# Queries, keys and values of tiles 4 to 7 made inside the loop's passes instead of in front, with other rings and buffers, in a one-core encoder block

## What is computed

```python
n1 = modulate(h, norm1_g, sh1, sc1)                  # 1024 tokens x 1024, RMSNorm and shift/scale from c
z, xbc, dtf, dtb, qkv, gate_ssd, gate_na = jnp.split(n1 @ w_in, IN_OFFSETS, axis=-1)
y_ssd = ssd_branch(z, xbc, dtf, dtb, ...) @ w_ssd_br # conv, chunked scan in both directions, gated RMSNorm
y_na = neighbourhood_attention(q, k, v, na_rpb) @ w_na_br   # 16 heads of 64, window 8 x 16 on a 16 x 64 grid
mixed = jax.nn.sigmoid(gate_ssd) * y_ssd + jax.nn.sigmoid(gate_na) * y_na
h = h + g1 * (mixed @ w_out)
n2 = modulate(h, norm2_g, sh2, sc2)
# PEER: 8 heads x 16 experts for each token, out of 16384 rows of 1024 floats in u and as many in v
h = h + g2 * einsum(gate * gelu(u[eidx] . n2), v[eidx])
```

## Time and profile before

| | before |
|---|---|
| median of 3 runs | 4299.2 us (4278.68 to 4303.11) |
| the profiled execution, its own time | 4317.7 us |
| its span | 4316.0 us |
| TensorE busy, mean granted clock | 2867.7 us, 0.811 |
| VectorE busy | 2480.9 us |
| GpSimd busy | 2102.6 us |
| ScalarE busy | 807.9 us |
| moved by DMA | 1389.46 MB |

### The profile page before, as it was taken

How to read it: one execution, slowest core, us unless ns; L and a number is a source line. 1 busy time by engine, 2 the same in 40 slices (tenths; PEclk the granted TensorE clock), 3 DMA queues, 4 the chain that set the end, 5 groups by cost and what they waited for, 6 DMA issues and landing times.

```text
span 4316.0 us, 41932 instructions
## 1 busy us (share of the span) xinstructions
PE 2867.7 (66%) x14107; PEld 1470.9 (34%) x14107; DVE 2480.9 (57%) x5249; ACT 807.9 (19%) x1840; POOL 2102.6 (49%) x2147
## 2 busy tenths in 40 slices
PE   5999998997766677795565767365568752333334
PEld 4887775543333333332232223132223320000000
DVE  4543447338575556547755565677556666666651
ACT  3323123211123211212232001121320110000000
POOL 1000313014564455656654556666555566666665
PEclk8999999999877888997687988677879876665556
DMA  8425754549998899999987999999899999999998
GB/s 212 66 65 172 227 169 153 196 177 378 393 322 323 294 403 406 405 407 377 371 332 286 403 405 405 406 355 366 308 347 404 402 392 364 372 369 368 377 367 333
DMA packets 503878, 1389.46 MB, mean 322 GB/s; under 512 B 65865, under 2 KB 136497, under 8 KB 502641
## 3 DMA queue, kind: packets, MB, share of 16 engines
q0 software_dynamic: 298768, 1086.75, 67.0%
q1 hardware_dynamic: 204896, 300.02, 20.2%
HBM read 1330.10 MB, written 56.51 MB: 321 GB/s over the span
## 4 chain that ended last, share of the span: by engine, by line
PE 21%; DMA 17%; POOL 13%; issue 12%; another core or an unknown queue 8%; DVE 7%; ACT 1%; SPq 0%; DVEq 0%; ACTq 0%; POOLq 0%
DMA ring<-in_peer_u,idx 13%; PE ps_l L1659 9%; POOL ring L2297 6%; POOL ring L2290 6%; PE acc L2519 4%; DVE junkF L2473 3%; DMA ring<-in_peer_v,idxT 2%; PE ps_l L1841 2%; PE ps_l L1887 1%; PE ps_l L1865 1%; DMA lane<-n_scr 1%; DMA gin<-zg_scr 1%; PE ps_l L1874 1%; PE ps_l L1734 1%
## 5 line engine op out<-in xcount | busy, mean ns | idle before, releaser
L2473 DVE CUSTOM_DVE_ANT_0 junkF<-ring,ps_n2F 128x1024 bf16<-128x1024 f32 x1024 | 1248.5, 1219 | 833.0 <-DMA ring<-in_peer_u,idx 585.1
L2297 POOL DMA_INDIRECT ring<-in_peer_u,idx x1024 | 1001.0, 978 | 877.3 <-DVE dots L2473 410.5
L2519 PE MATMUL acc<-ring,spread 128*32 128x512 f32 x4096 | 743.8, 850 | 911.7 <-DMA ring<-in_peer_v,idxT 772.1
L2290 POOL DMA_INDIRECT ring<-in_peer_v,idxT x1024 | 990.5, 967 | 705.3 <-PE acc L2519 286.8
L1659 PE MATMUL ps_l<-lane 128*128 128x512 f32 x1856 | 834.9, 604 | 41.7 <-DMA lane<-n_scr 18.8
L2519 PEld LDWEIGHTS acc<-ring,spread 128*32 128x32 f32 x4096 | 147.6, 138 | 1395.8 <-issue 1392.3
L1659 PEld LDWEIGHTS ps_l<-lane 128*128 128x128 f32 x1856 | 350.4, 193 | 499.4 <-issue 495.4
L1887 PE MATMUL ps_l<-ident,st 128*128 128x128 f32 x448 | 87.0, 327 | 181.5 <-ACT lane L1918 141.7
L2019 DVE CUSTOM_DVE_ANT_0 st<-ps_l,lane 128x512 f32<-128x512 f32 x96 | 66.3, 690 | 230.6 <-PE ps_l L1841 180.0
L515 POOL DMA_DIRECT2D bias<-rpb_scr x16 | 13.2, 829 | 325.5 <-PE ps_dt L801 279.8
L1841 PE MATMUL ps_l<-lane 128*128 128x512 f32 x192 | 134.6, 791 | 26.4 <-DVE nmax L2019 26.4
(11 more groups left out here) (354 smaller groups left out, 3980.9 us busy)
## 6 DMA issues: line engine op xcount, KB each, us to landing
lane<-in_peer_wq SPq DMA_DIRECT2D x16, 2048.0 KB
lane<-in_w_in SPq DMA_DIRECT2D x14, 2048.0 KB
w_z<-in_w_in SPq DMA_DIRECT2D x16, 1024.0 KB, 6.1
adaB<-in_w_ada SPq DMA_DIRECT2D x16, 1024.0 KB
lane<-in_w_na_br SPq DMA_DIRECT2D x8, 2048.0 KB
lane<-in_w_ssd_br SPq DMA_DIRECT2D x8, 2048.0 KB
lane<-in_w_out SPq DMA_DIRECT2D x8, 2048.0 KB
ring<-in_peer_u,idx POOLq DMA_INDIRECT x1024
```

Of the source, the lines that this page charges most:

```text
L2290: pool.indirect_dma_start(v_rows[:, nv % RV, :], None, a["peer_v"][0], bass.IndirectOffsetOnAxis(ap=idxT[:, m % 2, col:col + 1], axis=0)). ...
L2297: pool.indirect_dma_start(u_rows[:, n % RU, :], None, a["peer_u"][0], bass.IndirectOffsetOnAxis(ap=idx[:, i % RI, j:j + 1], axis=0)).then_ ...
L2473: nc.vector.tensor_tensor_reduce(out=junk[:, :], in0=u_rows[:, n % RU, :], in1=ps_n[:, :], scale=1.0, scalar=0.0, op0=ALU.mult, op1=ALU.ad ...
L2519: last = nc.tensor.matmul(acc[q * QUAD:(q + 1) * QUAD, cols], spread[:, m % 2, c0:c0 + QUAD], v_rows[:, nv % RV, cols], start=(g == 0 and ...
```

## The change

In front, the values are made for tiles 0 to 3 only (8 items instead of 16) and the queries and keys for the first 512 tokens only (one half of 24 matmuls for each of the 16 blocks, and a store of 512 columns instead of 1024). What is missing becomes "mul" jobs of the loop's gate stages: in pass 1 the keys and values of tiles 4 and 5 (8 jobs, 4 weight blocks, and one more load of a normed tile), in pass 2 the queries of tiles 4 and 5 and the keys and values of tiles 6 and 7 (12 jobs, 6 blocks), in pass 3 the queries of tiles 6 and 7 (4 jobs, 2 blocks). Each job ends with a ScalarE copy and a 256 KB store in rows of 128 floats. Queries and keys are computed transposed, as 32 matmuls of 128 columns.

Four other things change. The first block of the SSD's x moves into `stage_condition`, between the steps that make `n1`; that stage has six rooms for w_ada instead of eight and two PSUM buffers instead of three. In the recurrence, the scaling of `ps_off` (one VectorE instruction, L1800) and the addition to y (one, L1809) leave VectorE: ScalarE does the first in 8 instructions of 64 columns and the second as a copy, and TensorE adds y itself by one more matmul. `junk` is gone: a dot product writes its products over its own u row and no longer waits for the one before. `prod`, `off` and `qrow` share a room with `st`, and the freed memory makes `RV` 11. The last steps of a tile (`finish_sum`, `finish_norm`) are spread over more slots.

With the same rule the slots become: pass 1 gate 14 to 84, recurrence 84 to 123, attention 123 to 174; pass 2 gate 244 to 328, recurrence 328 to 369, attention 369 to 426; pass 3 recurrence 572 to 616, attention 616 to 677.

```diff
+                ps_x0 = banks(front, "ps_x0", 2)
+                split_room = ExitStack()
+                x_order = [[opener(split_room)(f"w_x_{part}{i}", [P, KD, P], f32r) for part in ("hi", "lo")] for i in range(2)]
...
-        ada = sb("ada", [P, KD, 2 * DM])
+        ada = sb("ada", [P, ADA_ROOMS, 2 * DM])
...
+                    if k >= ADA_ROOMS:
+                        sp.wait_ge(ada_sum, ada_room(k) + 1)
+                    sp.dma_start(ada[:, ada_room(k), :], w_ada[:, k, 0:2 * DM]).then_inc(s_ada[k], 16)
+                for b in range(2):
+                    sp.dma_start(w_first[b], w_in[:, :, COL_XBC + b * P:COL_XBC + (b + 1) * P]).then_inc(s_wx[b], 16)
...
+                for b in range(2):
+                    act.wait_ge(s_wx[b], 16)
+                    nc.scalar.activation(x_order[b][0][:, :, :], w_first[b], ACT.Copy).then_inc(x_hi, 1)
...
-                v.wait_ge(sq_done, TT)
-                nc.vector.tensor_scalar(rstd[:, :], sumsq[:, :], 1.0 / DM, EPS, ALU.mult, ALU.add).then_inc(mean_done, 1)
-                v.wait_ge(sqrt_done, 1)
-                nc.vector.reciprocal(rstd[:, :], rstd[:, :]).then_inc(rstd_done, 1)
                 v.wait_ge(cT_done, 2)
                 for k in range(KD):
+                    if k == 1:
+                        v.wait_ge(sq_done, TT)
+                        nc.vector.tensor_scalar(rstd[:, :], sumsq[:, :], 1.0 / DM, EPS, ALU.mult, ALU.add).then_inc(mean_done, 1)
...
+                for k in range(KD + 3):
+                    if k == 2:
...
+                    q = k - 3
+                    if q >= 0:
+                        if q == 0:
+                            pe.wait_ge(x_lo, 1)
+                        pe.wait_ge(hi_done, q + 1)
+                        pe.wait_ge(lo_done, q + 1)
+                        for h in range(2):
+                            last = exact_products(nc, ps_x0[:, h * HALF:(h + 1) * HALF], lambda part, i: x_order[0][part][:, i, :],
+                                                  lambda part, i: n1[part][:, i, h * HALF:(h + 1) * HALF], [q])
...
+                last.then_inc(x_mm, 1)
...
-    GATE_BLOCKS = [(3, i, COL_V + i * HALF, ACT.Copy, TT) for i in range(2)]
+    GATE_BLOCKS = [(3, i, COL_V + i * HALF, ACT.Copy, TT // 2) for i in range(2)]
...
-                    sp.dma_start(qk_scr[b * P:(b + 1) * P, :], row[:, b % 2, :]).then_inc(s_row[b % 2], 16)
+                    early = slice(0, HALF)
+                    sp.dma_start(qk_scr[b * P:(b + 1) * P, early], row[:, b % 2, early]).then_inc(s_row[b % 2], 16)
...
-                for b in range(XBC_BLOCKS):
+                for b in range(1, XBC_BLOCKS):
...
-                    for half in range(2):
+                    for half in range(1):
...
-    RU, RV, RI = 6, 10, 2
+    RU, RV, RI = 6, 11, 2
...
-        junk = sb("junkF", [P, DM], bf16)
...
-        st_room = sb("st", [P, RS * (GRID_W + HALF)])
+        st_room = sb("st", [P, (RS + RQ) * HALF])
         st = st_room[:, 0:RS * HALF].rearrange("p (r n) -> p r n", r=RS)
-        probs = st_room[:, :].rearrange("p (r n) -> p r n", r=RS)
-        prod = sb("prod", [P, HALF])
-        qrow = sb("qrow", [P, RQ, HALF])
+        probs = st_room[:, 0:RS * (GRID_W + HALF)].rearrange("p (r n) -> p r n", r=RS)
+        prod = st_room[:, (RS - 1) * HALF:RS * HALF]
+        qrow = st_room[:, RS * HALF:].rearrange("p (r n) -> p r n", r=RQ)
         qcol = sb("qcol", [P, RQ, 4, P])
         lstat = sb("lstat", [P, 4])
         nmax = sb("nmax", [P, 2])
...
+        KEYED = {(2, 3): (4, 5), (4, 5): (6, 7)}
...
-                    + [("load", t) for t in held[SETS:]] + [("mul", "gate", c, t) for c in range(4) for t in gated])
+                    + [("mul", "query", c, t) for c in range(2) for t in tiles if t >= TT // 2]
+                    + [("load", t) for t in held[SETS:]] + [("mul", "gate", c, t) for c in range(4) for t in gated]
+                    + [("load", t) for t in KEYED.get(tiles, ()) if t not in held]
+                    + [("mul", what, c, t) for what in ("key", "value") for c in range(2) for t in KEYED.get(tiles, ())])
...
+                for k in [k for k, m in enumerate(st_jobs) if m < OPEN_AT[a_pass]][-RS:]:
+                    stored_wait(sp, k)
...
-                c, t = JOBS[n][2:]
-                sp.dma_start(zg_scr[1 + c // 2, t * P:(t + 1) * P, c % 2 * HALF:(c % 2 + 1) * HALF], st[:, k % RS, :]).then_inc(s_gst[k % RS], 16)
+                what, c, t = JOBS[n][1:]
+                dst, src = zg_scr[1 + c // 2, t * P:(t + 1) * P, c % 2 * HALF:(c % 2 + 1) * HALF], st[:, k % RS, :]
+                if what == "value":
+                    dst = v_scr[c * PAIRS // 2:(c + 1) * PAIRS // 2, :, t, :].rearrange("r q n -> q r n")
+                elif what in ("query", "key"):
+                    d0 = (DM if what == "key" else 0) + c * HALF
+                    dst = qk_scr[d0:d0 + HALF, t * P:(t + 1) * P].rearrange("(r q) n -> q r n", q=P)
+                if what != "gate":
+                    src = src.rearrange("q (r n) -> q r n", n=P)
+                sp.dma_start(dst, src).then_inc(s_gst[k % RS], 16)
 
...
+                if what in ("query", "key"):
+                    cols = slice(part * P, (part + 1) * P)
+                    for k in range(KD):
+                        last = nc.tensor.matmul(bank[:, cols], w[:, blk % RW, k, cols], inT[:, f % SETS, k, :], start=(k == 0), stop=(k == KD - 1))
...
+                pe.wait_ge(d_scaled, 3 * (t - SOON + 1))
+                y = tok[:, tok_of[turn_at(t, "y", 0)] % RT, :]
+                nc.tensor.matmul(ps_y, ident[:, :], y[:, g * GP:(g + 1) * GP], start=True, stop=False)
                 pe.wait_ge(d_offr, u + 1)
                 for d in range(2):
-                    nc.tensor.matmul(ps_y, ident[:, :], off[:, d * GP:(d + 1) * GP], start=(d == 0), stop=False)
+                    nc.tensor.matmul(ps_y, ident[:, :], off[:, d * GP:(d + 1) * GP], start=False, stop=False)
...
+            elif kind == "soff":
+                if u % (2 * GROUPS) == 0:
+                    for m in [m for m, n in enumerate(st_jobs) if n < JOBS.index(("soff", t, g))][-RS:]:
+                        stored_wait(act, m)
+                act.wait_ge(d_off, u + 1)
+                if u:
+                    act.wait_ge(d_y, u)
+                for d in range(2):
+                    for h in range(HPG):
+                        cols, col = slice(d * GP + h * HEADDIM, d * GP + (h + 1) * HEADDIM), d * SH + g * HPG + h
+                        last = nc.scalar.activation(off[:, cols], ps_off[:, cols], ACT.Copy, scale=tabs[:, t % 2, col:col + 1])
+                last.then_inc(d_offr, 1)
+            elif kind == "sy":
+                act.wait_ge(d_y, u + 1)
+                y = tok[:, tok_of[turn_at(t, "y", 0)] % RT, :]
+                nc.scalar.activation(y[:, g * GP:(g + 1) * GP], ps_y, ACT.Copy).then_inc(d_yr, 1)
...
+                if u:
+                    v.wait_ge(d_y, u)
...
-            elif kind == "sy":
-                v.wait_ge(d_y, u + 1)
-                v.wait_ge(d_scaled, 3 * (k + 1))
-                nc.vector.tensor_tensor(y[:, cols], y[:, cols], ps_y, ALU.add).then_inc(d_yr, 1)
...
+                what = JOBS[n][1]
+                if what == "gate":
+                    nc.scalar.activation(st[:, k % RS, :], bank, ACT.Sigmoid).then_inc(p_act, 1)
+                else:
+                    nc.scalar.activation(st[:, k % RS, :], bank, ACT.Copy, scale=-(HEADDIM ** -0.5) if what == "query" else 1.0).then_inc(p_act, 1)
...
-                            if n:
-                                v.wait_ge(u_used, n)
-                            nc.vector.tensor_tensor_reduce(out=junk[:, :], in0=u_rows[:, n % RU, :], in1=ps_n[:, :], scale=1.0, scalar=0.0,
+                            nc.vector.tensor_tensor_reduce(out=u_rows[:, n % RU, :], in0=u_rows[:, n % RU, :], in1=ps_n[:, :], scale=1.0, scalar=0.0,
...
-                        if i >= 1 and j == FIN_SLOT + 5:
+                        if i >= 1 and j == SQUARE_SLOT:
+                            finish_square(i - 1)
+                        if i >= 1 and j == NORM_SLOT:
...
+        SQUARE_SLOT, ROOT_SLOT, NORM_SLOT = FIN_SLOT + 3, FIN_SLOT + 4, FIN_SLOT + 7
```

More of the change, by code:

```diff
@@ L173, in ev_count, with evicted, ada_room @@
         def ev_count(k, by_act):
-            return sum((i % 3 == 1) == by_act for i in range(k + 1))
+            return sum((i % 2 == 1) == by_act for i in range(k + 1))
+        def evicted(engine, k):
+            engine.wait_ge(ev_act if k % 2 else ev_dve, ev_count(k, k % 2 == 1))
+        def ada_room(k):
+            return k if k < ADA_ROOMS else k - ADA_ROOMS + 1
         with nc.Block() as block:
@@ L334, in stage_front @@
             xT = sb("xT", [P, 2, SEQ])
-            x_order = [[sb(f"w_x_{part}{i}", [P, KD, P], f32r) for part in ("hi", "lo")] for i in range(RS)]
             x_parts = [[x_order[i][part] for i in range(RS)] for part in range(2)]
@@ L362, in stage_front @@
```

(7 more changed lines are left out.)

104 lines of the change are left out of this document (52 added, 52 removed).

## The result

The changed kernel takes **4340.5 us** (median of 4 runs, 4314.0 to 4363.6) against 4291.1 for the kernel before (4 runs, 4278.7 to 4303.1): ratio 1.010, 95% interval 1.0057 to 1.0143. Measured a second time (experiment 6), with 6 runs against 11, the same pair gave 1.0086 (1.0064 to 1.0108). I had forecast 4260 and a range of 4190 to 4330. The change is slower, and the forecast and its sign were wrong.

The account below looks back on a forecast made before the run. The prediction took the front as bound by TensorE and the loop by DMA; front -121 and loop +82 gave -39 us on the profiled 4317.7, 4278.7, hence 4260 us against the runs' median, range 4190 to 4330.

Parts of the forecast that it names:

- Values: Front: 8 items of 24 matmuls go, 192 x 0.2346 us, taken in full since TensorE is the bound: -45 us.
- First block: Front: the SSD x's first 48 matmuls fill gaps between the steps that make n1: -12 us (0 to -14).
- Queries and keys: Front's query loop: 384 matmuls leave, stage falls from 196.5 to 132 us: -64; ends -95 (TensorE bound), -30 (loads in turn).
- Bytes: Loop: 32.0 MB more of weight blocks, stores and one load cost DMA time: +90 us (79 to 110).
- TensorE: Loop's gate stages: 24 jobs bring TensorE level with DMA, so waits for each other show: +30 us (0 to +70).
- slots: Loop: attention loses 16 slots to gate stages, where each costs 0.7 us more: +12 us.
- The wait between dot products: Recurrence and attention: idling up to 0.30 us before dot products goes; a third of at most 88 us taken: -30 us.
- the 11th place: Loop's last window: GpSimd runs one v row further ahead, winning idle DMA time: -12 us (0 to -42).
- the recurrence: Recurrence stages: VectorE loses L1800 and L1809, ScalarE gets nine instructions instead: -8 us.
- rival A: Loop: 110 us of idle DMA time come back instead of 50, so the front's gain stays whole: 4200 us; chance 0.24.
- Rival B: Gate stages: SyncE's queue, with new stores in 512-byte rows, delays weights TensorE needs: slower, 4335 us; chance 0.14.
- Rival C: Front: query loop stays at 165 us, held by the load behind 1 MB of w_ada: 4293 us; chance 0.15.

Follow-up runs that it names:

- experiment 6: On one chip against the kernel before: the change again 1.0086; with 10 v-row places instead of 11, 1.0069; with the recurrence's offset product back on VectorE, 1.0124.
- experiment 7: The change with an eighth of each moved weight block loaded, 0.9933 of the kernel before; with two of eight matmuls per moved job, 1.0027.
- experiment 3: The change with queries, keys and values all back in front, 0.9952 of the kernel before; the same with ScalarE's copy before the split, 0.9939.
- experiment 2: The change with only the first eighth of each w_ada block in the query loop loaded and summed; single run, that stage 143.9 us, 185.0 in the change.
- experiment 1: The change with ScalarE copying query block b out before splitting block b + 2; 0.9993 of the kernel before, 4311.2 against 4318.9 us.

## Why the prediction was wrong, step by step

- **Values, -45:** right, -42.3. **First block, -12 (0 to -14):** -15.6; the next stage starts earlier by that. Right in kind, a little more than its end.
- **Queries and keys, -64 (ends -95 and -30): this step failed.** It was -17.9. I wrote "124 us, more than TensorE's 101, and I take 132, since the loads wait for one another in SyncE's order", and took as the bad end that "each block waits for its 1.5 MB in turn", at -30. That end is what happens, and it costs more than I gave it: 9.3 to 14.6 us a block, from one load's issue to the next. What I did not follow is ScalarE's order, by which the store, and with it the next load, waits for a later block's load. In the kernel before it was covered by some 11 us of matmuls a block (48 of 831 in 190.23 us), with 7 us of waits for a late split in all; halving the matmuls took the cover off, and TensorE's pauses between blocks came to 65 us. With the two lines swapped the stage took 140.6 us, 62 below before's 202.9: that is the -64. Of the 58 us missed, 46 are here and 12 in the loop; the rest nearly cancels (values +3, first block -4, the stages behind the query loop -2, the end +3).
- The rule of the Trainium skill ("DMA: Bandwidth & Descriptors", Specifications) that I had set against this, line rate at 512 bytes and more, is not borne out by this case. In the change's trace a packet of 512 bytes takes 27 ns (median), one of 1024 46, one of 2048 84 and one of 4096 160, so the shortest rows move at three quarters of the rate of the longest. The mended stage is at a share of 0.90 with only 256 GB/s, against 405 in gate stages; part of that is GpSimd's bias traffic, whose 4096-byte packets take 247 ns on average there. The -95 was out of reach besides: TensorE alone is busy 109 us in the mended stage.
- **Bytes, +90:** +83 in packet time; right. **TensorE, +30 and slots, +12:** pass 1's gate stage came to 248.9 us, I had said 225; its idle DMA time, against a share of 1.03, went from 6 to 31 us, so a cost of that size is there. But three quarters of the products left out bring only 12 us of the loop (experiment 7); that the rest is late loads is shown at one place and not summed up.
- **The wait between dot products -30, the 11th place -12, the recurrence -8: the sum of 50 failed.** Recurrences and attentions took 1091.1 us over 319 slots before and 1032.2 over 293 after. The 26 slots fewer are worth 59 us at the prediction's own 2.0 and 2.7 us a slot, and 59 is the difference: nothing is left for the three terms. The place gives nothing; wait and offset are perhaps 15 each by the times, with intervals that reach nearly down to nothing, and with nothing moved all the other parts together leave some 7 us in the loop (experiment 3). All three rest on one sentence: that the 178 us below a share of 1.03 are lost to late engines. Most are not, and the DMA engines' idle time grew by 13 us where the prediction's terms had it shrink by 8 (30 + 12 - 50).

To see that, the throughput in 5 us slices from 3700 to 3900 us, of the change and of experiment 2, whose code is the same there:

```profile
DMA  8999997999999799999999789999989999997999
GB/s 328 358 392 419 408 410 251 305 379 415 404 407 411 255 336 382 345 409 380 410 412 408 257 274 381 415 408 410 412 308 295 419 409 407 412 387 245 317 411 411
```
```profile
DMA  9999999999999999999899999999999999999999
GB/s 407 410 413 406 407 410 401 403 410 409 406 410 414 407 408 410 410 388 356 309 337 417 413 411 407 410 410 410 408 410 410 407 408 409 409 408 412 409 410 407
```

Where the change was profiled the flow breaks down to some 250 GB/s about every 35 us; on the faster chip once in the 200. There the attention of pass 2 and the last window read:

```profile
2070.00:2239.90 169.90, 129.69 (x1150) 63.29 (x1150) 119.94 (x320) 71.57 (x208) 107.11 (x113) 0.84 1.03 399
...
3298.60:3993.20 694.60, 243.31 (x1219) 54.43 (x1217) 454.25 (x1001) 42.84 (x100) 508.57 (x533) 0.58 1.02 406
```

The same program attends at a share of 1.03 where it had 0.90, with VectorE in the same order. Over the whole loop the idle time against 1.03 is 39 us there and 196 here. So VectorE's lateness was not what held those stages; freeing it had little to win. It falls with this that **rival A** (110 us of idle DMA time back) rested on the same reading. **Rival B** forecast the sign and 4335, by stores of 512-byte rows in SyncE's queue; pass 1's gate stage did come to 249, at its mark of 250. But its mechanism is not what the forecast missed: most of that lies in the front, and in the gate stage, with every store kept, the weights or products left out bring 16 and 8 us, while the 4096 store rows of 512 bytes take 27 ns each (median), 6.9 us over 16 engines. Its own mark for the run without the products, a stage above 240 us, was not met either (230.6, where the unaltered stage takes 238.5). What is right in it is that loads come late in SyncE's one queue. The stores themselves were not left out in a run. **Rival C**, "the front does not get shorter as said", was the right one, and its 165 us still too few: 185. The cause that it named is only a part of it: the w_ada in front is some 3 of 12 us a block.

## What to carry to other kernels

Before halving the work that hides a loop's loads, write down the cycle that is left: for each engine in order, which instruction the next load stands behind, and what that one waits for. A ring of two rooms says nothing while a copy stands behind the wait for a later load; here moving one line gave back 0.9%. And an idle share of DMA is no reserve until a run on another chip, or one with the suspected wait removed, shows that it moves.

## What the runs showed of the hardware

- The chip of experiments 2 and 7 differs from the others in DMA: the kernel before took 4291, 4319 and 4317 us on three occasions and 4093 there. A dot product takes 1.22 us on both, and the unaltered front is alike (experiment 2). In the loop, the same code but for what experiment 2 leaves out in front, the packets' time is 3213 us against 3278, and the idle time against a share of 1.03 is 39 against 196.
- The median 4096-byte packet of a gather is 160 ns in the change's trace and 162 on the fast chip, but of 265,280 such packets 5776 took over 300 ns in the change's trace (6066 before), and 2821 in experiment 2's; the longest took 2.3 us. In the change's trace nine tenths of them lie in a quarter of the loop's 5 us slices. Within these dips the DMA share falls to 0.73, so the engines also stand idle. What causes them was not tried, and stays open.
- A DMA share can read 1.03; a stage at 0.90 in which rows of 512 and 1024 bytes take 63% of the packets' time moved 256 GB/s (experiment 1), one at 1.03 with rows of 2048 and 4096 bytes 405.
- VectorE's low split of a query block takes 1.23 us when GpSimd runs no instruction of its bias work beside it, and 2.0 to 4.1 us when one (2.35 us each) overlaps it: 5 of 16 splits in the change's trace, 5 of 16 before, 4 of 16 with the copy first. TensorE waits for the split there; the next load does not.
